# Routing on 50 candidate pairs, and an up-projection in products of 448 columns whose halves VectorE adds

## The reference, cut to what matters

```python
q = (h @ w_q).reshape(B, S, 8, 2, 128)
sc = jnp.einsum('bshpd,phnd->bshpn', q, keys)          # 8 heads x 2 halves x 128 keys
v1, i1 = lax.top_k(sc[..., 0, :], 16)
v2, i2 = lax.top_k(sc[..., 1, :], 16)
cand = (v1[..., :, None] + v2[..., None, :])           # 16 x 16 sums
cidx = (i1[..., :, None] * 128 + i2[..., None, :])
best, pos = lax.top_k(cand, 16)
idx = jnp.take_along_axis(cidx, pos, axis=-1)
gates = jax.nn.softmax(best, axis=-1)
act = jax.nn.gelu(u[idx] @ h);  out = (gates * act) @ v[idx]
```

## Time and profile before

| | us |
|---|---|
| median of 3 runs | 1378.35 (1378.18 to 1378.45) |
| the profiled execution | 1378.15 |
| its span in the profile | 1376.1 |
| TensorE busy | 1357.4 (99%), granted clock 0.998 |
| VectorE, ScalarE, GpSimd busy | 1036.9, 737.2, 292.8 |
| up-projection's first 62 units | about 262 to 428 |

### The profile page before, as it was taken

One profiled execution on the slowest core, in us unless ns is written; L12 is line 12 of the kernel. 1 busy time (PEld: TensorE's weight loads), 2 busy tenths in 40 slices (PEclk: granted clock), 3 DMA queues, 4 the chain that ended last, 5 costly groups with the idle time before them and its releaser, 6 DMA issues.

```text
span 1376.1 us, 26736 instructions
## 1 busy us (share of the span) xinstructions
PE 1357.4 (99%) x10948; PEld 1290.1 (94%) x10949; DVE 1036.9 (75%) x1848; ACT 737.2 (54%) x1078; POOL 292.8 (21%) x176
## 2 busy tenths in 40 slices
PE   9999999999999999999999999999999999999997
PEld 7989989999999999999999999999998798899986
DVE  5556575593987899989999888887887664777744
ACT  5674645545464444444444456555677554655543
POOL 6000000388874222220000033320132000100001
PEclk9999999999999999999999999999999999999999
DMA  7443355455569777775555589986443543555552
GB/s 248 140 136 123 128 195 215 141 197 199 197 221 333 280 242 247 247 258 181 186 185 185 194 323 349 350 308 237 149 146 107 182 154 116 176 184 185 185 190 99
DMA packets 76585, 279.26 MB, mean 203 GB/s; under 512 B 8496, under 2 KB 8752, under 8 KB 76208
## 3 DMA queue, kind: packets, MB, share of 16 engines
q1 hardware_dynamic: 67104, 243.73, 51.5%
q0 software_dynamic: 9216, 33.56, 6.5%
q10 hardware_dynamic: 144, 0.26, 0.1%
HBM read 276.47 MB, written 1.05 MB: 202 GB/s over the span
## 4 chain that ended last, share of the span: by engine, by line
PE 89%; ACT 4%; DVE 4%; POOL 1%; issue 1%; DMA 0%; POOLq 0%; SPq 0%; DVEq 0%
PE bank L478 88%; ACT A L1232 2%; PE bank L487 1%; DVE wlo L1828 1%; ACT whi L1232 1%; DVE A L1828 1%; POOL wlo L2780 1%; ACT L1232 1%; DMA xres<-in_x 0%; DVE xres L1828 0%; DVE A L1824 0%; ACT hT L1232 0%; DVE small L2576 0%; DVE A L1825 0%; DVE small L1828 0%
## 5 line engine op out<-in xcount | busy, mean ns | idle before, releaser
L478 PE MATMUL bank<-hT,whi 128*128 128x224 f32 (+2 forms) x5148 | 1008.7, 293 | 2.6 <-DVE wlo L1828 1.7
L478 PEld LDWEIGHTS bank<-hT,whi 128*128 128x128 f32 x5148 | 811.4, 190 | 18.8 <-DVE wlo L1828 2.5
L478 PE MATMUL bank<-hT,wlo 128*128 128x224 f32 (+1 forms) x2952 | 810.8, 275 | 0.0
L1232 ACT ACTIVATE whi<-raw 128x1024 fp32r<-128x1024 f32 (+1 forms) x450 | 473.1, 1054 | 352.2 <-PE bank L478 344.5
L1828 DVE TENSOR_TENSOR wlo<-raw,whi 128x1024 fp32r<-128x1024 f32 (+1 forms) x386 | 472.9, 1226 | 226.3 <-ACT whi L1232 226.0
L478 PEld LDWEIGHTS bank<-hT,wlo 128*128 128x128 f32 x2952 | 562.6, 191 | 0.0
L1232 ACT ACTIVATE A<-bank 128x512 f32<-128x512 f32 (+4 forms) x170 | 90.2, 537 | 213.1 <-PE bank L478 203.5
L2780 POOL TENSOR_TENSOR wlo<-raw,whi 128x1024 fp32r<-128x1024 f32 x62 | 148.6, 2414 | 111.9 <-ACT whi L1232 109.4
L2796 POOL DMA_INDIRECT A<-in_v,small x32 | 50.5, 1578 | 288.1 <-DVE A L1824 174.1
L2796 POOL DMA_INDIRECT A<-in_utab,small x32 | 54.5, 1704 | 132.5 <-DVE A L1831 131.0
L2786 POOL TENSOR_TENSOR small<-small 128x1 f32<-128x1 f32 x14 | 8.3, 594 | 339.8 <-DVE small L1825 336.7
(11 more groups left out here) (183 smaller groups left out, 1327.4 us busy)
## 6 DMA issues: line engine op xcount, KB each, us to landing
raw<-in_u SPq DMA_DIRECT2D x128, 512.0 KB, 3.3
raw<-in_v SPq DMA_DIRECT2D x128, 512.0 KB, 3.6
raw<-in_w_up SPq DMA_DIRECT2D x44, 512.0 KB, 3.2
raw<-in_w_down SPq DMA_DIRECT2D x22, 512.0 KB, 3.3
raw<-in_w_in_t SPq DMA_DIRECT2D x17, 512.0 KB, 4.0
raw<-in_w_in_g SPq DMA_DIRECT2D x16, 512.0 KB, 3.2
raw<-in_w_out SPq DMA_DIRECT2D x16, 512.0 KB, 3.6
raw<-in_w_pq SPq DMA_DIRECT2D x16, 512.0 KB, 3.6
```

What stands on the lines that cost most here:

```text
L478: return e.matmul(o, l, r, start=st, stop=sp_, skip_group_check=True)
L1232: return e.activation(o, i, func, **kw)
```

## The change

Two parts, both beside each other in the first 62 units.

Routing: the 16 best sums of two sorted lists of 16 lie among the pairs (i, j) with (i + 1)(j + 1) <= 16, which are 50. Only these sums are made (seven blocks), searched and decoded. The decoding is another: for a position, the first-list rank is the number of starts passed (`first16`, by `is_ge`), and a sum over `pay` (key number steps plus 256 x row length) gives key number and offset in one; a piece of five short dependent instructions takes them apart. Pieces per block stay 30; the second search has 5 pieces where it had 10, the decoding more.

Up-projection: units 2 to 49 (`wide`) multiply the high weights with high and low activations in one product of 448 columns, and the low weights with the high activations in one of 224. Each unit has a bank of its own. ScalarE copies columns 224 to 447 out (`take_low`, to `og`), VectorE adds them to columns 0 to 223 (`add_low`), ScalarE applies gelu in place on pairs. VectorE's addition of unit u-1 stands ahead of the piece of routing at unit u.

```diff
+BEST_OF = [16 // (i + 1) for i in range(16)]
+NBEST = sum(BEST_OF)
+BEST_BLOCKS = [(0, 1, 16), (1, 1, 8), (2, 1, 5), (3, 1, 4), (4, 1, 3), (5, 3, 2), (8, 8, 1)]
+WIDE = (2, 50)
...
+        def u_part(n):
+            return og[:, 2 * TD * (n % 2):2 * TD * (n % 2 + 1)].bitcast(F32)
+
+        def is_wide(n):
+            return WIDE[0] <= n < WIDE[1]
...
+            def wide(u0, u1, steps):
+                both = t4(hT[:, :], 2, KD)
+                for u in range(u0, u1):
+                    i = BASE["u"] + u
+                    wv = two(unit(i), KD)
+                    b = 4 + (u - 1) % 3
+                    use(b)
+                    for k in range(KD):
+                        mm(banks[b][:, 0:2 * TD], wv[0][:, k, :], both[:, :, k, NG:T], k == 0, False)
+                        ins = mm(banks[b][:, 0:TD], wv[1][:, k, :], both[:, 0, k, NG:T], False, k == KD - 1)
+                        if 2 * (k + 1) == KD:
+                            mid.step()
+                    ins.then_inc(s["w"], 1)
+                    free[b] = (s["u_sum"], u - WIDE[0] + 1)
+                    pair[0] += u % 2
                     side.step(steps[(i + 1) % len(steps)])
...
-            lin_T(BASE["u"], 62, hTv, KD, steps=U1_STEPS, c0=NG)
+            lin_T(BASE["u"], WIDE[0], hTv, KD, steps=U1_STEPS, c0=NG)
+            wide(*WIDE, U1_STEPS)
+            lin_T(BASE["u"] + WIDE[1], 62 - WIDE[1], hTv, KD, steps=U1_STEPS, c0=NG)
...
-                for _ in range(21):
+                for _ in range(19):
                     yield
                 e.wait_ge(s["rt_dve"], 4 * b + 1)
                 act(bex, bex, ACT.Exp).then_inc(s["rt_act"], 1)
                 yield
-                for _ in range(8):
+                for _ in range(10):
...
-            lin_T(BASE["u"], 62, gelu(0), rep_h, steps=U1_STEPS)
+            def take_low(n):
+                if n - 2 >= WIDE[0]:
+                    e.wait_ge(s["u_sum"], n - 1 - WIDE[0])
+                e.wait_ge(s["w"], BASE["u"] + n + 1)
+                act(u_part(n), banks[4 + (n - 1) % 3][:, TD:2 * TD], ACT.Copy).then_inc(s["u_low"], 1)
+
+            for u in range(62):
+                hi(BASE["u"] + u + 2)
+                if is_wide(u - 1):
+                    take_low(u - 1)
+                if u % 2 and is_wide(u - 3):
+                    e.wait_ge(s["u_sum"], u - 1 - WIDE[0])
+                    z = acts[:, u - 3:u - 1, :]
+                    act(z, z, ACT.Gelu).then_inc(s["ev_act"], 1)
+                    pair[0] += 1
+                if u % 2 and not is_wide(u):
+                    e.wait_ge(s["w"], BASE["u"] + u + 1)
+                    gelu(u - 1)(0, t3(banks[4 + pair[0] % 3][:, :], 2))
+                    pair[0] += 1
+                rep_h(u)
+                side.step(U1_STEPS[(BASE["u"] + u + 1) % len(U1_STEPS)])
...
-                shape = [P, 8, 16, 16]
                 v2p = t3(banks[7][:, 16:16 + P], 8)
+                pay = t3(candw[:, 8 * NBEST:8 * NBEST + P], 8)
                 own(e.tensor_copy(v2p, vv[:, :, 1, :]))
                 again()
-                own(tt(t4(cand, 8, 16), vv[:, :, 0, :].unsqueeze(3).to_broadcast(shape),
-                       v2p.unsqueeze(2).to_broadcast(shape), ALU.add))
+                own(e.tensor_copy(pay[:, :, 0:1], iv[:, :, 0, 0:1]))
+                own(tt(pay[:, :, 1:16], iv[:, :, 0, 1:16], iv[:, :, 0, 0:15], ALU.subtract))
+                at = 0
+                c50, w50 = (t3(z[:, 0:8 * NBEST], 8) for z in (cand, candw))
+                for i, n, w in BEST_BLOCKS:
+                    shape = [P, 8, n, w]
+                    own(tt(c50[:, :, at:at + n * w].rearrange("p h (n w) -> p h n w", n=n),
+                           vv[:, :, 0, i:i + n].unsqueeze(3).to_broadcast(shape),
+                           v2p[:, :, 0:w].unsqueeze(2).to_broadcast(shape), ALU.add))
+                    at += n * w
+                again()
+                own(tt(pay, pay, banks[7][:, 160:176].unsqueeze(1).to_broadcast([P, 8, 16]), ALU.add))
                 yield
                 bv = t3(best, 8)
                 pu = t3(posu[:, 0:128], 8).bitcast(U32)
-                yield from top16(t3(cand, 8), t3(candw, 8), bv, pu, 8, 4)
-                pall = posu[:, 0:128].bitcast(U32)
-                again()
-                ts(posu[:, 128:256].bitcast(U32), pall, 4, None, ALU.logical_shift_right)
-                own(ts(posu[:, 256:384].bitcast(U32), pall, 15, None, ALU.bitwise_and))
-                again()
-                own(e.tensor_copy(posf, posu[:, 128:384].bitcast(U32)))
+                yield from top16(c50, w50, bv, pu, 8, 8)
+                again()
+                own(e.tensor_copy(posf[:, 0:P], posu[:, 0:P].bitcast(U32)))
                 tt(t3(bex, 8), bv, bv[:, :, 0:1].to_broadcast([P, 8, 16]), ALU.subtract).then_inc(s["rt_dve"], 1)
                 yield
+                part = [P, 2, 16, 16]
                 for q in range(2):
                     ps = t3(posf[:, q * P:(q + 1) * P], 8)
-                    part = [P, 2, 16, 16]
-                    again()
-                    for g in range(4):
-                        own(tt(t4(banks[g][:, :], 2, 16), ps[:, 2 * g:2 * g + 2, :].unsqueeze(3).to_broadcast(part),
-                               banks[7][:, 0:16].unsqueeze(1).unsqueeze(1).to_broadcast(part), ALU.is_equal))
-                    again()
-                    for g in range(4):
-                        own(tt(t4(oh2[:, g * 512:(g + 1) * 512], 2, 16), t4(banks[g][:, :], 2, 16),
-                               iv[:, 2 * g:2 * g + 2, q, :].unsqueeze(2).to_broadcast(part), ALU.mult))
-                    yield
-                    again()
-                    own(e.tensor_reduce(t3(sel_i[q], 8), t4(oh2, 8, 16), AX, ALU.add))
-                    yield
+                    ref = (banks[7][:, 144:160], banks[7][:, 0:16])[q].unsqueeze(1).unsqueeze(1).to_broadcast(part)
+                    worth = iv[:, :, 1, :] if q else pay
+                    dst = sel_i[1] if q else scw[:, 400:528]
+                    for h in range(2):
+                        again()
+                        for g in (2 * h, 2 * h + 1):
+                            own(tt(t4(banks[g][:, :], 2, 16), ps[:, 2 * g:2 * g + 2, :].unsqueeze(3).to_broadcast(part),
+                                   ref, ALU.is_equal if q else ALU.is_ge))
+                        again()
+                        for g in (2 * h, 2 * h + 1):
+                            own(tt(t4(oh2[:, g * 512:(g + 1) * 512], 2, 16), t4(banks[g][:, :], 2, 16),
+                                   worth[:, 2 * g:2 * g + 2, :].unsqueeze(2).to_broadcast(part), ALU.mult))
+                            if g == 2 * h:
+                                yield
+                        again()
+                        own(e.tensor_reduce(t3(dst[:, 64 * h:64 * h + 64], 4),
+                                            t4(oh2[:, 1024 * h:1024 * h + 1024], 4, 16), AX, ALU.add))
+                        yield
+                    if q == 0:
+                        pi = posu[:, P:2 * P].bitcast(U32)
+                        again()
+                        own(e.tensor_copy(pi, dst))
+                        again()
+                        own(ts(posu[:, 2 * P:3 * P].bitcast(U32), pi, 8, None, ALU.logical_shift_right))
+                        again()
+                        own(e.tensor_copy(posf[:, P:2 * P], posu[:, 2 * P:3 * P].bitcast(U32)))
+                        again()
+                        own(stt(sel_i[0], posf[:, P:2 * P], -256.0, dst, ALU.mult, ALU.add))
+                        again()
+                        own(tt(posf[:, P:2 * P], posf[:, 0:P], posf[:, P:2 * P], ALU.subtract))
+                        yield
...
+            def add_low(u):
+                n = u - 1
+                if is_wide(n):
+                    e.wait_ge(s["u_low"], n - WIDE[0] + 1)
+                    tt(acts[:, n, :], banks[4 + (n - 1) % 3][:, 0:TD], u_part(n), ALU.add).then_inc(s["u_sum"], 1)
+                pick_u(u)
+
+            lin_T(BASE["u"], 62, before=add_low, steps=U1_STEPS)
```

More of the change, by code:

```diff
@@ L77 @@
     ("ident", 128), ("g_mix", 8), ("g_ffn", 8), ("g_mix2", 8), ("g_x2", 8), ("g_mem2", 8), ("g_ffn2", 8),
-    ("iota", 128), ("iota16", 16),
+    ("iota", 128), ("iota16", 16), ("first16", 16), ("steps16", 16),
     ("cfw", 66), ("cfb", 22), ("pick", NG),
@@ L172 @@
 own_act own_dve own_pool zeros x_sq hi_half lo_half lo_first f_xd f_act hd_mask
-pk_idx pk_rep pk_used pk_act v_tile v_b v_sum v_tr x_g
+pk_idx pk_rep pk_used pk_act v_tile v_b v_sum v_tr u_low u_sum x_g
 """.split()
@@ L628, in lin_T @@
                         after(u)
+                    side.step(steps[(i + 1) % len(steps)])
+            def wide(u0, u1, steps):
[13 more added lines that the diff above has]
+                    pair[0] += u % 2
                     side.step(steps[(i + 1) % len(steps)])
@@ L2665, in dve_program @@
             own(e.tensor_copy(banks[7][:, 0:16], K_("iota16")))
```

(6 more changed lines are left out.)

## The result

The changed kernel took 1392.98 us, median of five runs (1392.20 to 1395.01); the one before, run beside it, 1378.18 us (1377.99 to 1378.45). The ratio is 1.011, 95% interval 1.0097 to 1.0124: **14.8 us slower**. The prediction had the sign, and 3.6 us in place of 14.8; its range ended at 1388.

The account below looks back on a forecast made before the run. TensorE, busy 99% of the span, bounds the kernel. Gain -7.2 us, stalls +11.0 and the old stall -0.2 make +3.6 us on the profiled execution, given as 1382.0 us; range 1371.5 to 1388.

Parts of the forecast that it names:

- TensorE's gain: Up-projection units 2 to 49: a 448- and a 224-column product replace three of 224, saving 0.15 us per unit, 7.2 us.
- rival D: The 448-column product is cheaper in the wide units than in the down-projection: gain 15 us, total 1374; chance 0.02.
- ScalarE and VectorE's added work at nothing: Wide units: ScalarE's 0.36 us copies and VectorE's 17 us of additions, offset by 18 us shorter routing, cost nothing themselves.
- The slack of 3.1 us: Wide units: VectorE may fall 3.1 us behind in all before TensorE waits for an addition, needed before unit n+3.
- the chain of five: Decoding beside units 20 and 48: five dependent VectorE instructions each wait for one whole GpSimd subtraction; block 0 stalls 4.3 us.
- the tables: Piece building block 0's tables, beside unit 27: 14 instructions that wait for GpSimd make the addition late, stall 3.0 us.
- the low parts: After block 1's decoding beside unit 48, VectorE's low parts of the weights from unit 54 come late: 3.5 us.
- the sums: Pieces with the 50 sums, beside units 10 and 38: the addition lands slightly late, 0.1 us of stall each.
- Rival A: VectorE's waits for GpSimd don't chain in the wide units: stalls of 0 to 2 us, total 1372; chance 0.22.
- B: Two VectorE instructions get through per subtraction boundary: stalls of about 6 us in all, total 1377; chance 0.08.
- C: Lateness feeds itself after a stall, so sums, tables and decoding all stall: 18 us, total 1389; chance 0.06.
- Also at nothing: Constants' transfer grows by 32 columns, first read a whole stage after landing; no other DMA changes: cost nothing.

Follow-up runs that it names:

- allfree: The changed kernel with the five decoding instructions, the 50 sums and the gate tables freed of SBUF-only instructions by use of PSUM: 1377.87 us, ratio 0.9997.
- allfree32: The kernel of allfree with 32 more unused columns among the constants, hT 256 bytes from its place before the change: 1373.08 us, ratio 0.9960.
- Chain: The changed kernel with only the five dependent decoding instructions per block given an operand or result in PSUM: 1383.71 us, ratio 1.0037.
- warm: The changed kernel with 40 dummy products of zeros put into TensorE's wait ahead of unit 23: 1393.71 us, ratio 1.0116.
- wideonly: The changed kernel with the old routing of 256 sums kept under the wide units: 1395.97 us, ratio 1.0125.

## Why the prediction was right, and where it failed

- **TensorE's gain, 7.2 us: right at this place.** 7.4 from the stage's account; 7.7 from allfree, whose stage is 7.1 us shorter with 0.6 us more of waiting than before. The k-steps are the forecast ones outside the slow stretches (0.315 us). But it is no constant: 256 bytes on (allfree32) the stage gains 5.4 us. That the sum went by 0.21 us of the earlier trace rows and not by the 0.19 us of the Trainium skill ("TensorE: Matmul & The Clock Gate", Back-to-back issue gap) was right; rival D is out.
- **ScalarE and VectorE's added work at nothing: right.** No wait of TensorE in the stage is for ScalarE.
- **The slack of 3.1 us and the chain of five: right.** Four of the five waited for a subtraction or its rest, and the fifth ran when none was left, as forecast. Stall 5.0 for 4.3 forecast, 2.9 for 3.0 at the tables, 2.6 for 3.5 at the low parts, 0.6 twice for 0.1 twice at the sums, with the last 0.2 us 11.9 for 11.0. That the sum came so near is in part luck: the decoding of block 0 and the sums were too low, the low parts too high. Chain and allfree remove them by the very operands that were blamed. Rival A (waits don't chain) and B (two per boundary) are out; so is C (lateness feeding itself), for no stall fed another.
- **Beside unit 48** only three of the five were locked (the gather's issue breaks the row), as the step said:

```profile
403.69 2.32 DVE L2228 CAST A<-A 128x128 f32<-128x128 uint32 x1
406.05 0.29 DVE L1880 SCALAR_TENSOR_TENSOR A<-A 128x128 f32<-128x128 f32 x1
```

  The wait that followed, 2.6 us, lies under the stated 2.7 to 4.9.

- **The rule on the shared port pair** (the Trainium skill, "SBUF — State Buffer", Who interferes with whom), of which no trace then showed the dependent case, holds here: four instructions of 1.98 to 2.33 us against an unbroken row of subtractions, 0.28 to 0.30 us once one side lies in PSUM.
- **"Also at nothing" failed: 6.7 us.** The step asked when the constants' transfer lands, and not what 32 more columns push along: pad32 has these columns alone and takes 6.7 us more. It was the largest single term missing.
- **The price of a stall failed: 3.4 us.** The sum counted the idle time alone. TensorE's clock fell behind two of the waits. In the trace of before TensorE had no wait of that length in the stage, so no row there priced it; it should have stood in the sum as an open bound.
- Small slips without weight: stalls of 18 us give 1389, the last line has 1388; the gain by the shorter product is some 16 us in one place and 15 in the other.
- The sum then: 3.6 + 0.9 (stalls) - 0.15 (the old gap, 0.35 and not 0.2) + 3.4 (clock) + 7.2 (outside the stage) - 0.2 (gain) = 14.75, measured 14.8. It closes because the gain of 7.4 us is the remainder of the stage's account; with allfree's 7.7 it would be 14.45. Either missing term alone takes the time past 1382.0; the place alone takes it to 1388.7, beyond the range.

## What to carry to other kernels

A row of dependent instructions is priced by what each of them may have to wait for, not by its busy time; where GpSimd runs without gaps beside it, an operand or result in PSUM brought each here from about 2.3 us back to 0.3. Before two kernels are compared on a few tenths of a per cent, pad one so that the operands of the long loops lie at the same place in both, and try two or three places: they were worth as much here as the change itself. A stall on TensorE is counted with the slow products that may follow it.

## What the runs showed of the hardware

- **The address of the moving operand tells.** With `hT` 128 bytes on, a 256-column product with `whi` goes from 334.1 / 1840 to 338.3 / 1840 us, 1.3% busier, and a 448-column one from 248.7 to 250.9 us per 756. At 192 and 256 bytes the 256-column ones are back. The 448-column ones differ by stage, from start to start in the traces: in the down-projection (620 to 880 us) 215 ns at 0, 220 at 128, 216 at 192 and at 256 bytes; in the wide units 213 at 128, 211 at 192, 219 at 256. The 224-column ones of the up-projection don't move at 128. At 32 bytes the 256-column ones lose and the 512-column ones that read other buffers gain (395 to 390 ns of modelled length). What decides, the runs don't say.
- **The clock after idling.** 4.85 us of idling: k-steps at 0.59 us for five steps, then 0.315, 1.7 us lost. 2.5 us at 415: 1.7 us lost in the change, nothing in warm. 2.7 us at unit 30: nothing in the change, 1.7 us lost behind the same wait in chain and in warm, where no slow stretch had come 20 us earlier. In wideonly one had (from 334.6 us), and slow products followed the wait that ended at 348.77 all the same. Neither the length of the wait nor an earlier slow stretch tells alone.
- **VectorE's strided copy of 128x8** waits like the others beside a subtraction:

```profile
291.41 2.05 DVE L2173 CAST A<-A 128x256 f32<-128x256 uint32 x1
293.69 2.17 DVE L2180 COPY A<-A 128x8 f32<-128x8 f32 x1
```
